# Routing from unscaled rows in halves, one K = 96 product for the down bias, the up bias in row halves

## The reference, cut to what matters

```python
h = h + mix @ w_out                        # 512 x 1024, w_out 1024 x 1024
xn = rmsnorm(h, norm_ffn_g)                # h * rsqrt(mean(h * h) + 1e-5) * g
logits = xn @ w_router + b_router          # 1024 x 32
top_v, top_i = lax.top_k(logits, 4)
gates = softmax(top_v)
# for each token and each of its experts e:
hdn = xn @ w1[e] + b1[e]                   # 1024 x 2048: gate half, linear half
gate = minimum(hdn[:1024], 7)
lin = clip(hdn[1024:], -7, 7)
act = gate * sigmoid(1.702 * gate) * (lin + 1)
h += gates[e] * (act @ w2[e] + b2[e])      # w2 1024 x 1024
out = rmsnorm(h, norm_final_g)
```

## Time and profile before

| | |
|---|---|
| median of three timed runs | 2038.61 us (2032.73 to 2038.63) |
| the profiled execution, whole | 2029.47 us |
| its span, which all rows refer to | 2027.7 us |
| mean granted clock of TensorE | 0.984 of full |
| TensorE busy | 1962.6 us, 97% |
| VectorE busy | 1558.4 us, 77% |
| ScalarE busy | 1219.1 us, 60% |
| GpSimd busy | 233.9 us, 12% |
| DMA | 540.16 MB, 266 GB/s on the mean |

### The profile page before, as it was taken

The page is one execution under the profiler, slowest core; times in us unless marked ns, Lnnn a source line. Parts: engine busy times, 40 slices in busy tenths (PEclk is TensorE's granted clock), DMA queues, the critical chain, the costliest instruction groups (busy, mean ns, idle before and its releaser), DMA issues.

```text
span 2027.7 us, 25897 instructions
## 1 busy us (share of the span) xinstructions
PE 1962.6 (97%) x9234; PEld 1599.4 (79%) x9234; DVE 1558.4 (77%) x1499; ACT 1219.1 (60%) x1064; POOL 233.9 (12%) x175
## 2 busy tenths in 40 slices
PE   7998989999999999999999999999999999999998
PEld 5776777777777888768888888888888888888886
DVE  6654447878775226479989899999989999898987
ACT  6544434536344213347777777777777777777776
POOL 0000204352612000101000000000000000000000
PEclk8999999999999999889999999999999999999999
DMA  5132434343525935379999999999999999999995
GB/s 148 45 104 84 145 103 158 94 156 119 161 73 187 339 99 172 150 287 371 384 369 379 368 378 370 372 381 366 381 365 376 371 371 383 366 380 367 376 363 195
DMA packets 211717, 540.16 MB, mean 266 GB/s; under 512 B 16339, under 2 KB 131445, under 8 KB 174728
## 3 DMA queue, kind: packets, MB, share of 16 engines
q1 hardware_dynamic: 204368, 518.46, 69.9%
q0 software_dynamic: 7056, 20.80, 4.5%
q10 hardware_dynamic: 232, 0.08, 0.0%
HBM read 512.08 MB, written 31.20 MB: 268 GB/s over the span
## 4 chain that ended last, share of the span: by engine, by line
PE 68%; DVE 2%; DMA 1%; SPq 1%; issue 0%; ACT 0%; ACTq 0%; DVEq 0%
PE ps L1822 35%; PE ps L1882 16%; PE ps L244 3%; PE ps L246 3%; PE ps L245 3%; PE ps L1815 2%; PE ps L1790 1%; PE ps L1855 1%; PE ps L1985 1%; SPq L2251 1%; DMA ssd_low<-ssd_out_T 1%; DVE temps L1269 1%; PE ps L1611 1%; PE ps L1737 0%; PE ps L1087 0%
## 5 line engine op out<-in xcount | busy, mean ns | idle before, releaser
L1720 DVE TENSOR_TENSOR w_low<-ring_b,w_high 128x2048 fp32r<-128x2048 f32 x192 | 437.1, 2287 | 49.0 <-ACT w_high L1714 46.8
L1720 DVE TENSOR_TENSOR w_low<-ring_a,w_high 128x2048 fp32r<-128x2048 f32 x192 | 436.9, 2287 | 48.2 <-ACT w_high L1714 45.9
L1714 ACT ACTIVATE w_high<-ring_a 128x2048 fp32r<-128x2048 f32 x192 | 368.5, 1920 | 152.5 <-PE ps L1822 116.5
L1714 ACT ACTIVATE w_high<-ring_b 128x2048 fp32r<-128x2048 f32 x192 | 368.6, 1920 | 145.4 <-PE ps L1822 108.6
L1822 PE MATMUL ps<-w_high,rows_high 128*128 128x512 f32 x1024 | 403.3, 394 | 0.1
L1822 PE MATMUL ps<-w_high,rows_low 128*128 128x512 f32 x1024 | 400.4, 391 | 0.0
L1822 PE MATMUL ps<-w_low,rows_high 128*128 128x512 f32 x1024 | 399.7, 390 | 0.0
L1822 PEld LDWEIGHTS ps<-w_high,rows_high 128*128 128x128 f32 x1024 | 193.0, 189 | 42.2 <-DVE w_low L1720 2.5
L1822 PEld LDWEIGHTS ps<-w_high,rows_low 128*128 128x128 f32 x1024 | 192.8, 188 | 41.0
L1822 PEld LDWEIGHTS ps<-w_low,rows_high 128*128 128x128 f32 x1024 | 193.0, 189 | 39.9
L239 DVE TENSOR_TENSOR unit_low<-unit_raw,unit_high 128x1024 fp32r<-128x1024 f32 x108 | 142.4, 1328 | 97.1 <-ACT unit_high L234 97.0
(11 more groups left out here) (379 smaller groups left out, 2870.5 us busy)
## 6 DMA issues: line engine op xcount, KB each, us to landing
ring_a<-in_w SPq DMA_DIRECT2D x192, 1024.0 KB, 7.5
ring_b<-in_w SPq DMA_DIRECT2D x192, 1024.0 KB, 7.5
unit_raw<-in_w_in SPq DMA_DIRECT2D x80, 512.0 KB, 4.0
temps<-cum_rows SPq DMA_DIRECT2D x16, 1024.0 KB, 7.4
unit_raw<-in_w_up_ssd SPq DMA_DIRECT2D x16, 512.0 KB, 7.8
ssd_out_T<-y_high SPq DMA_DIRECT2D x4, 1024.0 KB, 6.3
ssd_out_T<-y_low SPq DMA_DIRECT2D x4, 1024.0 KB, 6.6
ssd_high<-ssd_out_T SPq DMA_DIRECT2D x4, 1024.0 KB, 11.3
```

The lines of the kernel that those rows point to most:

```text
L1714: nc.scalar.activation(w_hi[:, split_at(it, j)], slot(at, 1)[:, 0, :], ACT.Copy).then_inc(w_hi_ok, 1)
L1720: nc.vector.tensor_tensor(w_lo[:, split_at(it, j)], slot(at, 1)[:, 0, :], w_hi[:, split_at(it, j)].bitcast(F32), ALU.subtract).then_inc(w_ ...
```

## The change

- **Routing.** `rows_T` and `route` work in halves of four chunks. What is transposed is `h3`, the rows before normalisation; the norm's gain is multiplied into the router weights once, and the reciprocal root of a token is applied to its logits in `pick_rows`. The first halves' transposes stand ahead of piece 1 of j = 1, the second half's in the middle of later pieces, and the routing products with them. The static parts of `slot_of` and the small index ramps are made earlier. `pick_rows(0)` and `(1)` stand behind the normalised rows of tiles 2 and 3, the other two behind them.
- **Down bias.** Gates and b2 are split into high and low parts, stacked to 96 rows (gates high, high, low against b2 high, low, high), and each 128 x 512 piece is one fp32r product over K = 96. Tile 0 stands behind the first `rows_pe`, tiles 1 and 2 inside the up products of pass 0, tile 3 behind the `rows_pe` at its end. All use banks 4 and 5. b2 is loaded three times. The stores of rows are spread over the loads of pass 1.
- **Up bias.** `b1_s` has 1024 columns: the gate half on partitions 0 to 63 (high, low), the linear half with its +1 on 64 to 127. Each of the four products contracts over 64 rows; the order is gate half, linear half, gate half, linear half. b1 is loaded in four parts.
- In pass 1 `acts_pe(0)` stands behind the second weight tile and the slot products behind the fourth.

```diff
 
-        def out_piece(pe, n):
+        def out_piece(pe, n, chunks=range(NK)):
 
             _, j, t = pieces[n]
...
-            for k in range(NK):
+            for k in chunks:
                 pe.wait_ge(mix_lo_ok, k + 1)
                 still = tuple(chunk(a, k)[:, tokens(t)] for a in (mixT_hi, mixT_lo))
                 last = three(ps[:, 2 * t + j, :], still, (four(w[0], k), four(w[1], k)), k == 0, k == NK - 1)
-            last.then_inc(h_ps, 1)
-
-        def rows_T(pe, t):
-            pe.wait_ge(h_v, t + 1)
-            for c in range(NK):
-                last = nc.tensor.transpose(ps[:, 2 * t + c // 4, (c % 4) * P:(c % 4 + 1) * P], f_n[:, t, c * P:(c + 1) * P], ident[:])
+            if k == NK - 1:
+                last.then_inc(h_ps, 1)
+
+        THREE = 3 * NE
+        FIRST, SECOND = range(0, NK // 2), range(NK // 2, NK)
+
+        def rows_T(pe, t, half):
+            pe.wait_ge(h_ok, half * NT + t + 1)
+            for c in (FIRST, SECOND)[half]:
+                last = nc.tensor.transpose(ps[:, 2 * t + half, (c % 4) * P:(c % 4 + 1) * P], h3[:, t, c * P:(c + 1) * P], ident[:])
             last.then_inc(fT_ps, 1)
 
-        def route(pe, t):
-            pe.wait_ge(gf_in, 32)
-            pe.wait_ge(fT_ok, t + 1)
-            for k in range(NK):
+        def route(pe, t, half):
+            pe.wait_ge(lg_ok, 1)
+            pe.wait_ge(fT_ok, half * NT + t + 1)
+            for k in (FIRST, SECOND)[half]:
                 last = nc.tensor.matmul(ps[:, 2 * t, 0:NE], f_T[:, k, tokens(t)], wr_w[:, k, :], start=k == 0, stop=k == NK - 1)
-            last.then_inc(lg_ps, 1)
...
 
         def bias_pe(pe, t):
 
-            if t == 0:
-                pe.wait_ge(b_in, 16)
-                pe.wait_ge(rt_a, 2)
-            if t == 1:
-                pe.wait_ge(rt_v, MOST_OK)
-            a = (0, 2, 4, 0)[t]
+            if t:
+                pe.wait_ge(h_ok, 2 * NT + t)
+            else:
+                pe.wait_ge(b2_lo, b2_lo0 + 2)
             for n in range(2):
-                last = nc.tensor.matmul(ps[:, a + n, :], g_T[0:NE, tokens(t)], b2_w[0:NE, n * 512:(n + 1) * 512], start=True, stop=True)
+                last = nc.tensor.matmul(ps[:, 4 + n, :], g_T[0:THREE, tokens(t)], b2_s[0:THREE, n * 512:(n + 1) * 512], start=True, stop=True)
             last.then_inc(rt_ps, 1)
+
+        def bias_low_dve(v):
+
+            v.wait_ge(rt_a, 2)
+            gate_low, b2_low = slice(2 * NE, 3 * NE), slice(NE, 2 * NE)
+            nc.vector.tensor_tensor(g_T[gate_low, :], ps[gate_low, 5, :], g_T[gate_low, :].bitcast(F32), ALU.subtract).then_inc(b2_lo, 1)
+            v.wait_ge(b2_hi, b2_hi0 + 1)
+            nc.vector.tensor_tensor(b2_s[b2_low, :], b2_w[b2_low, :], b2_s[b2_low, :].bitcast(F32), ALU.subtract).then_inc(b2_lo, 1)
 
         def bias_dve(v, t):
             v.wait_ge(rt_ps, 4 + t)
-            a = (0, 2, 4, 0)[t]
             ht = h3[:, t, :].rearrange("p (a b) -> p a b", a=2)
-            nc.vector.tensor_tensor(ht, ht, ps[:, a:a + 2, :], ALU.add).then_inc(h_ok, 1)
+            nc.vector.tensor_tensor(ht, ht, ps[:, 4:6, :], ALU.add).then_inc(h_ok, 1)
 
...
             else:
                 pe.wait_ge(silu_ok, it)
                 pe.wait_ge(lin_ok, it)
-            if isinstance(it, int) and it == 1:
-                pe.wait_ge(h_ok, 3 * NT)
-            for n in range(4):
-                nc.tensor.matmul(ps[:, n, :], pick[:, :], b1_s[:, n * 512:(n + 1) * 512], start=True, stop=False)
+            for n in range(2):
+                for half in range(2):
+                    rows = slice(half * 2 * NE, (half + 1) * 2 * NE)
+                    nc.tensor.matmul(ps[:, 2 * half + n, :], pick[rows, :], b1_s[rows, n * 512:(n + 1) * 512], start=True, stop=False)
             for k in range(UP):
                 pe.wait_ge(w_lo_ok, tile_no(it, k) + 1)
                 at = split_at(it, k).start
@@ -1821,7 +1837,11 @@
                     for i, (a, w) in enumerate(((rows_hi, w_hi), (rows_hi, w_lo), (rows_lo, w_hi))):
                         last = nc.tensor.matmul(ps[:, n, :], a[:, k, :], w[:, cols], start=False, stop=k == UP - 1 and i == 2)
                 last.then_inc(w_used, 1)
-                if k == 2 and more:
+                if is_first(it) and k in (3, 6):
+                    bias_pe(pe, k // 3)
+                if isinstance(it, int) and it == 1 and k == 1:
+                    acts_pe(pe, 0)
+                if k == (3 if isinstance(it, int) and it == 1 else 2) and more:
                     if not is_first(it):
                         pe.wait_ge(a_lo_ok, it)
...
         def down_pe(pe, it, first):
 
             pe.wait_ge(a_lo_ok, it)
-            if not (isinstance(it, int) and it == 1):
+            if isinstance(it, int) and it == 1:
+                pe.wait_ge(h_ok, 3 * NT)
+            else:
                 pe.wait_ge(ye_ok, it - 1)
             for u in range(DOWN):
...
             up_pe(pe, it, odd, more)
             rows_pe(pe, it + 1, 1 - odd, more)
             if is_first(it):
-                bias_pe(pe, 2)
-                pe.wait_ge(silu_ok, 1)
                 bias_pe(pe, 3)
             else:
                 down_pe(pe, it, UP)
-            acts_pe(pe, it)
+                acts_pe(pe, it)
 
         def pass_act(act, it, odd):
...
                 tokens_dve(v, it + 2)
                 slots_dve(v, it + 3)
             pick_dve(v, it + 1)
+            if is_first(it):
+                bias_dve(v, 1)
             for j in range(6, UP):
                 low_dve(v, it, odd, j)
-            if not is_first(it):
+            if is_first(it):
+                bias_dve(v, 2)
+            else:
                 for j in range(UP, UP + 2):
                     low_dve(v, it, odd, j)
             linear_dve(v, it)
@@ -1946,7 +1970,6 @@
             glu_dve(v, it)
             if is_first(it):
                 bias_dve(v, 3)
-                bias_dve(v, 2)
 
         sel_T = at("sel_T", AT_H3 + D, SEQ, F32R)
...
 
         def experts_sync(sp):
             store_rows(sp, 0)
-            store_rows(sp, 1)
             for j in range(UP):
                 load_tile(sp, 1, 1, j)
-            sp.wait_ge(h_ok, 3 * NT)
-            store_rows(sp, 2)
-            store_rows(sp, 3)
+                if j in (3, 5, 7):
+                    store_rows(sp, j // 2)
             for j in range(UP, TILES):
                 load_tile(sp, 1, 1, j)
...
             nc.scalar.activation(flat(e_all), flat(e_all), ACT.Exp).then_inc(rt_a, 1)
             high_act(act, 0, 0, 1)
             act.wait_ge(rt_ps, 3)
-            nc.scalar.activation(g_T[0:NE, :], ps[0:NE, 5, :], ACT.Copy).then_inc(rt_a, 1)
+            nc.scalar.activation(g_T[0:THREE, :], ps[0:THREE, 5, :], ACT.Copy).then_inc(rt_a, 1)
+            act.wait_ge(b_in, 48)
+            act.wait_ge(h_sq, 2 * NT)
...
         def experts_vector(v):
             tokens_dve(v, 0)
             slots_dve(v, 1)
+            bias_low_dve(v)
             low_dve(v, 0, 0, 0)
             tokens_dve(v, 1)
             slots_dve(v, 2)
             pick_dve(v, 0)
+            rows_dve(v, 0)
             bias_dve(v, 0)
-            bias_dve(v, 1)
-            rows_dve(v, 0)
...
             sp.wait_ge(h_ps, NT)
-            for half in range(2):
-                sp.dma_start(b1_rows[half * NE:(half + 1) * NE, :], b1).then_inc(b1_in, 16)
+            for part in range(4):
+                cols = slice(part // 2 * DFF, (part // 2 + 1) * DFF)
+                sp.dma_start(b1_rows[part * NE:(part + 1) * NE, :], b1[:, cols]).then_inc(b1_in, 16)
             for t in range(NT):
                 sp.wait_ge(h_v, t + 1)
                 sp.dma_start(xn_d[t * P:(t + 1) * P, :], f_n[:, t, :]).then_inc(f_out, 16)
-            sp.dma_start(b2_w[0:NE, :], b2).then_inc(b_in, 16)
+            for part in range(3):
+                sp.dma_start(b2_w[part * NE:(part + 1) * NE, :], b2).then_inc(b_in, 16)
...
             for t in range(NT):
                 out_piece(pe, N_OUT + t)
             out_piece(pe, N_OUT + NT)
-            out_piece(pe, N_OUT + NT + 1)
-            rows_T(pe, 0)
-            out_piece(pe, N_OUT + NT + 2)
-            rows_T(pe, 1)
-            out_piece(pe, N_OUT + NT + 3)
-            rows_T(pe, 2)
-            route(pe, 0)
-            route(pe, 1)
-            rows_T(pe, 3)
-            route(pe, 2)
-            route(pe, 3)
+            for t in range(NT):
+                rows_T(pe, t, 0)
+            for t in range(1, NT):
+                out_piece(pe, N_OUT + NT + t, FIRST)
+                rows_T(pe, t - 1, 1)
+                if t == 1:
+                    for u in range(NT):
+                        route(pe, u, 0)
+                else:
+                    route(pe, t - 2, 1)
+                out_piece(pe, N_OUT + NT + t, SECOND)
+            route(pe, NT - 2, 1)
+            rows_T(pe, NT - 1, 1)
+            route(pe, NT - 1, 1)
...
```

(41 more changed lines are left out.)

105 lines of the change are left out of this document (56 added, 49 removed).

## The result

Twelve runs of each kernel on one chip: **2039.76 us** (2037.01 to 2042.42) for the changed kernel, 2033.34 us (2031.05 to 2038.63) for the one before. The ratio is 1.003, 95% interval 1.0021 to 1.004, so the change costs about 6 us. I had forecast 1.5 us less than before, which I called no change that can be measured. The profiled executions have spans of 2038.0 and 2027.7 us, 10.3 apart, of which 2.4 arose ahead of the changed stretch: the add of piece 3 of j = 0 begins at 820.29, for 817.87 before. In the ten experiments, which leave that part alone, it lies between 817.47 and 821.13, so this is spread.

The account below looks back on a forecast made before the run. TensorE was taken to bound the kernel nearly throughout. Routing +5.5, gather to end of pass 0 -0.8, transition +1.9 and up bias -8.1 gave -1.5 us: 2038.61 to 2037.1 us, range 2029 to 2047.

Parts of the forecast that it names:

- part 3: Up bias in row halves, steady passes: two halves run together, gaining 0.27 us a pass, -8.1 in 30 passes.
- full drain: Case for the two tiling changes in each pass: 0.16 us each, gain 0.17 a pass, sum +1.5 instead of -1.5.
- Part 1: Routing in halves around the last output piece: routing ends 5.5 us late, bounds +4 and +7.
- the routing delay isn't there: Rival at the routing: the picks hide, then -7 us; counted within a rival of chance 0.22.
- The gather: Fetching pass 0's rows once the indices are ready: forecast to take no longer than before, change 0.
- the start is dearer: Rival: the later gather meets the second four weight tiles, or pass 1's clock is low twice; +3 to +8, chance 0.11.
- Pass 0: First expert pass: two down-bias tiles inside add 0.9 us, slow clock 0.5; its up products end 4.7 late.
- The transition: From pass 0's up products to the end of pass 1's: +1.9 us, middle of +1.1 and +2.7, with a 2.4 stall.
- The base: Median of three timed runs, 2038.61 us, to which the forecast difference of -1.5 us was applied.

Follow-up runs that it names:

- e5: Changed kernel with all four up-bias products over rows 0 to 63, the linear half's bias left out: 2053.8 us, ratio 1.0104.
- e3: Changed kernel with the second up-bias pair moved behind the first three weight products, so each pass enters and leaves 64-row form twice: 2053.99 us, ratio 1.0109.
- e2: Changed kernel with both up-bias products of rows 0 to 63 first, then both of rows 64 to 127: 2040.82 us, ratio 1.0044.
- e4: Kernel before with only the up bias in row halves, routing and down bias as before: 2030.83 us, ratio 0.9994.
- e6: Changed kernel with pass 0's activations transposed at the end of pass 0 again, slot products behind pass 1's third tile: 2036.16 us, ratio 1.0021.
- e8: Changed kernel with whole-tile routing in the order of before and all four picks behind the last normalised rows: 2032.55 us, ratio 1.0002.
- e9: Changed kernel with the edits of e8 and e6 together: 2028.99 us, ratio 0.9984.
- e1: Changed kernel with the up bias over all 128 rows again, routing and down bias as changed: 2043.51 us, ratio 1.006.
- e10: e9 with the up bias over all 128 rows again: 2031.25 us, ratio 0.9989.
- e7: Changed kernel with the second four weight tiles loaded ahead of the last tile's row store and the down-bias loads: 2039.92 us, ratio 1.0037.

## Why the prediction was wrong

**The step that failed is part 3**, the term of -8.1 us. Its mechanism held: 64-row products of two halves run together, the four cost two pitches (0.66 - 0.20 = 0.46), and within one half they don't (e5, 1.12). Its size was off. I wrote 0.95 - 0.46 - 0.20 and took 0.20 for both switches: 0.09 on the way in and 0.11 on the way out. Both are there, 0.10 and 0.11 in e3. What the sum left out is a third part, the 0.20 between the last pair's pitch and the first weight product (0.66 - 0.46 in the changed kernel, 0.43 - 0.23 in e3). In and out is 0.39 to 0.41. That leaves 0.95 - 0.46 - 0.39 = 0.10. Six kernels with the halves (e2, e4, e6, e8 and e9 beside the changed one) run a mean pass of 35.357 to 35.385 us, three without (before, e1, e10) one of 35.448 to 35.460: 0.08 between the means, 2.4 us in all and not 8.1. e7 has the halves too and its mean pass is 35.44, (1976.60 - 948.91) / 29, but that is one pass: its usual pass is 35.35, as in the changed kernel, and one takes 36.97. In that one an indirect DMA on the residual rows took 10.71 us, for 8.2 to 9.6 in the ten passes around it, VectorE had to wait for it, and TensorE for VectorE (chain of waits and TensorE, e7):

```profile
1908.73 10.71 DMA residual_rows<-late_b
...
1923.71 0.50 PE L1838 MATMUL ps<-w_high,rows_high 128*128 128x512 f32 x1 [1.32 <-DVE w_low L1736]
```

The misreading was of the earlier trace rows: the 0.09 and 0.11 came from two different excursions, one going in and one coming out, and each was read at the product next to the switch, so that nothing was counted in between. There I should have asked for a whole stretch, from a known pitch to a known pitch.

The Trainium skill, page "TensorEngine Tiling (Array Packing)", section Key Properties, says that a change of tiling mode drains TensorE. The runs fit it: the weight load behind the pairs starts with its product (950.52) and not 0.24 ahead, and each of the two changes costs about 0.19 us (half of e3's 0.39), more than the 0.16 that I had called a full drain. With 0.16 each the sum was +1.5 us, the nearer one, and I should have given it more weight than two rows of other shapes.

**Part 1** held: +5.2 for +5.5. The last add moved by 6.9 (forecast 6.5), and 1.7 were won behind it (forecast 1.0), so two small misses cancel. TensorE accounts for 6.6 of that: the last product of the last piece starts at 850.23, 29.94 after the reference add, for 841.17 and 23.30 before. The other 0.3 is VectorE, which has the first pick (849.11 on) ahead of the last add and takes that add up without a pause. Three picks stand behind the last tile's rows (854.32, 855.97, 857.61, a pitch of 1.64 for 1.59). e8 gives 5.0 back. The rival "the routing delay isn't there" is out.

**The gather** was the part of a rival, "the start is dearer", that came true: +1.7, which the sum had at nothing. The second four weight tiles were issued at 856.55 for 845.88, 8.3 later by the reference add, since SP's queue had the last row store and two more bias loads ahead of them, and the indices only 5.2 later. So the gather came 7.4 us behind the first of them and no longer 10.5. I had counted 0.9 for the bias loads on top of the +5.5 of the indices. But the last row store waits for the last rows and not for the picks, and those rows end 7.0 later (VectorE's 853.12 + 1.28 for 843.73 + 1.28, by the reference add), so that the tiles come late by 7.0 + 0.9 and more. The rival named the collision; the sum put no price on it.

**Pass 0**: bias in it +0.96 as forecast (0.9). The slow clock cost 1.3 and not 0.5: the 36 products took 10.17 for 8.87, with the clock at 0.50 until 880 and 0.84 in 880 to 882, so that it rose some 5 us behind the first up bias at 875.69. Before, it rose in 870 to 872 behind one at 867.44. Why it took longer isn't shown.

```profile
878.00:880.00 2.00, 2.00 (x7) 1.52 (x6) 2.00 (x2) 0.00 (x0) 0.00 (x0) 0.50 0.84 236
880.00:882.00 2.00, 2.00 (x9) 1.65 (x8) 1.81 (x7) 0.29 (x1) 0.00 (x0) 0.84 0.86 348
```

(Windows of the changed kernel, columns as above.)

**The transition** held in kind: ScalarE's fourth high half (919.04) stands behind the eviction of the activations, and TensorE loses 2.4 us ahead of the fourth tile, as forecast. The size, +2.4 for +1.9, came near by luck. The +1.9 was the middle between a stall alone (+1.1) and a stall that drops the clock again (+2.7), and the clock stayed at 1.00 from 918 to 924. The 1.3 above the +1.1 arose mostly ahead of the stall: the first two tiles took 8.27 us for the 4.4 + 2.75 of the forecast. The clock was at 0.50 in 908 to 910 and still in 912 to 914, with the first product at 909.37; before, it was at 0.54 already in 898 to 900 and back at 0.76 in 904 to 906, with the first product at 901.33, so more of the slow stretch passed in waiting. e6 removes the stall and ends 0.9 below the kernel before (32.25 for 33.12).

**The base.** I applied the difference to a median of three runs, 2038.61; twelve runs give 2033.34. Against 2038.61 the result would have looked like +1. The ratio of runs on one chip is what counts, and by it I was off by 6.4 + 1.5 = 7.9 us. That 2039.76 lies only 2.7 above the 2037.1 that I wrote down is the luck of that base. The two profiled executions have 5.8 in the passes and 3.1 in the start, 1.0 more than the medians; single executions of one kernel differ by more than that.

## What to carry to other kernels

Work in smaller pieces between other work pays if the consumer's queue can take the pieces early. Here it couldn't: all that TensorE did ahead of the last output piece was paid in full, and VectorE's in-order queue kept three of four picks behind the last rows. Price a change of tiling by the whole stretch between two undisturbed pitches, in and out together, and make an excursion worth it or have only one. When an issue order moves a large load and a small gather by different amounts, compute their new distance. And behind each moved wait look for the eviction that it holds up.

## What was not expected

- Products over rows 0 to 63 and 64 to 127 overlap in either order of issue: 0.66 us for A, B, A, B and for A, A, B, B, but 1.12 if all lie in one half.
- Entering and leaving a 64-row stretch costs 0.39 us together (e3), for fp32r products of 512 columns.
- The granted clock can fall while TensorE never idles. In e1 it was 0.62 and then 0.50 from 832 on, right behind sixteen routing products (32 records) of 32 columns, with PE busy 2.00 of 2.00 us in each window; the changed kernel's own profile shows 1.00 in the same place. Of the six other builds with half routing all but e3 show it: their last add began 32.04 to 34.28 after the reference add, against 30.47 in e3 and 30.48 in the changed kernel. In the kernels with whole tiles the same add lies at 23.55 to 23.57. It comes in some executions and not in others; what decides it wasn't tried.
